# Attention on one core: more buffers behind the reciprocals and the outputs, the next head's loads spread over the groups, another order on TensorE

## What is computed

```python
def fox_attend(q, k, v, cq, ck, pos_q, pos_k):
    scale = HEAD_DIM ** -0.5
    s = jnp.einsum('bqhd,bkhd->bhqk', q, k).astype(jnp.float32) * scale
    decay = jnp.transpose(cq, (0, 2, 1))[:, :, :, None] - jnp.transpose(ck, (0, 2, 1))[:, :, None, :]
    mask = pos_k[None, :] <= pos_q[:, None]
    s = jnp.where(mask[None, None], s + decay, NEG_INF)
    p = jax.nn.softmax(s, axis=-1)
    return jnp.einsum('bhqk,bkhd->bqhd', p.astype(v.dtype), v)
...
    merged = jnp.concatenate([rms_norm(o_attn, g_attn_out), rms_norm(o_conv, g_conv_out)], axis=-1)
    x = x + rms_norm(merged @ w_o, g_post_mix)
```

## Time and profile before

| | us |
|---|---|
| median of 3 runs | 2822.99 |
| lowest, highest | 2822.49, 2825.99 |
| the profiled execution, its own time | 2823.09 |
| its span, first to last instruction | 2821.3 |
| PE busy in the span | 2691.7 (95%) |
| DVE, ACT, POOL busy | 1523.6, 1116.0, 1422.2 |
| granted TensorE clock, mean | 0.981 |

### The profile page before, as it was taken

How to read it: one execution, slowest core, us unless ns; L and a number is a source line. 1 busy time by engine, 2 the same in 40 slices (tenths; PEclk the granted TensorE clock), 3 DMA queues, 4 the chain that set the end, 5 groups by cost and what they waited for, 6 DMA issues and landing times.

```text
span 2821.3 us, 41366 instructions
## 1 busy us (share of the span) xinstructions
PE 2691.7 (95%) x14796; PEld 2403.9 (85%) x14796; DVE 1523.6 (54%) x2594; ACT 1116.0 (40%) x2065; POOL 1422.2 (50%) x912
## 2 busy tenths in 40 slices
PE   9999999998788888999999999999999999999998
PEld 8999999997666667788889898888988898889986
DVE  5333433347666668566533434655655565555554
ACT  3201201117666666544423333443333344333333
POOL 3233334311323322577467777765665577656664
PEclk9999999999899899999999999999999999999999
DMA  6634535664554543467735446621122163221213
GB/s 200 196 108 130 167 96 161 205 174 116 137 149 128 145 134 119 155 208 201 225 116 189 170 147 213 241 90 59 65 68 74 59 261 120 66 68 59 74 59 105
DMA packets 295665, 385.17 MB, mean 137 GB/s; under 512 B 24744, under 2 KB 240752, under 8 KB 291440
## 3 DMA queue, kind: packets, MB, share of 16 engines
q1 hardware_dynamic: 256352, 328.68, 37.8%
q0 software_dynamic: 13920, 35.13, 3.7%
q10 hardware_dynamic: 25264, 19.66, 2.2%
HBM read 276.76 MB, written 106.40 MB: 136 GB/s over the span
## 4 chain that ended last, share of the span: by engine, by line
PE 45%; POOL 2%; DVE 1%; DMA 1%; issue 1%; ACT 0%; SPq 0%; DVEq 0%; POOLq 0%
PE dn_bank L2969 17%; PE up_bank L2945 14%; PE dn_bank L2925 7%; PE up_bank L2900 7%; POOL m_y L2480 1%; POOL m_w_up L2429 1%; DMA m_raw_up<-in_w_up 0%; DMA m_x<-scratch_x 0%; DVE m_raw_up L2721 0%; DVE m_y L2826 0%; DVE m_t L2721 0%; POOL m_u L2472 0%; ACT m_junk L2622 0%; DVE m_y L2780 0%; POOL m_w_dn L2465 0%
## 5 line engine op out<-in xcount | busy, mean ns | idle before, releaser
L2969 PE MATMUL dn_bank<-m_w_dn,m_u 128*128 128x512 f32 x2304 | 542.4, 395 | 1.6 <-POOL m_w_dn L2465 1.6
L2969 PEld LDWEIGHTS dn_bank<-m_w_dn,m_u 128*128 128x128 f32 x2304 | 432.3, 188 | 103.6 <-POOL m_w_dn L2465 1.9
L2945 PE MATMUL up_bank<-m_h,m_w_up 128*128 128x384 f32 x2688 | 472.7, 336 | 7.5 <-DVE m_stage L2735 4.4
L2945 PEld LDWEIGHTS up_bank<-m_h,m_w_up 128*128 128x128 f32 x2688 | 467.1, 188 | 11.7 <-issue 5.0
L2782 DVE TENSOR_TENSOR m_y<-dn_bank,m_y 128x1024 f32<-128x1024 f32 x168 | 205.8, 1225 | 283.1 <-PE dn_bank L2969 283.1
L509 POOL TENSOR_TENSOR w_lo<-w_raw,w_hi 128x1024 fp32r<-128x1024 f32 x72 | 175.8, 2446 | 343.0 <-DVE w_hi L723 343.0
L2472 POOL TENSOR_TENSOR m_u<-m_stage,m_u 128x384 fp32r<-128x384 f32 x128 | 141.5, 1126 | 290.5 <-ACT m_u L2611 290.5
L2429 POOL TENSOR_TENSOR m_w_up<-m_raw_up,m_w_up 128x512 fp32r<-128x512 f32 x128 | 192.3, 1522 | 62.7 <-ACT m_w_up L2579 62.7
L1439 ACT ACTIVATE p_hi<-t_bank 128x512 fp32r<-128x512 f32 (+1 forms) x336 | 167.6, 527 | 137.8 <-PE t_bank L1526 94.2
L939 PE MATMUL proj<-ha_hi,w_hi 128*128 128x384 f32 (+1 forms) x640 | 212.2, 332 | 0.0
L1490 DVE TENSOR_TENSOR p_lo<-t_bank,p_hi 128x512 fp32r<-128x512 f32 (+1 forms) x336 | 189.1, 596 | 39.3 <-ACT p_hi L1439 38.2
(11 more groups left out here) (291 smaller groups left out, 5844.3 us busy)
## 6 DMA issues: line engine op xcount, KB each, us to landing
m_raw_up<-in_w_up SPq DMA_DIRECT2D x48, 1024.0 KB, 5.3
m_raw_dn<-in_w_down SPq DMA_DIRECT2D x47, 1024.0 KB, 4.9
w_raw<-in_w_in SPq DMA_DIRECT2D x72, 512.0 KB, 4.0
scratch_h_pairs<-m_pieces POOLq DMA_DIRECT2D x12, 1792.0 KB, 8.4
m_h<-scratch_h_pairs SPq DMA_DIRECT2D x14, 1536.0 KB, 11.8
nck<-scratch_ncum SPq DMA_DIRECT2D x8, 1312.0 KB, 7.9
scratch_v_hl<-vhl SPq DMA_DIRECT2D x20, 512.0 KB, 2.7
q_hi<-scratch_q_hi SPq DMA_DIRECT2D x16, 528.0 KB, 7.5
```

Of the source, the lines that this page charges most:

```text
L2945: mm = pe.matmul(out, w_up[:, j, wp, k, :], hidden_rows(g, j, hp, k), start=(k == 0 and p == 0), stop=(k == KH - 1 and p == 2))
L2969: mm = pe.matmul(bank[:, cols], part, wd[:, wp, b, cols], start=(b == 0 and p == 0), stop=(b == 1 and p == len(passes) - 1))
```

## The change

`o_t` and the scales get four buffers by using both halves of the 128 partitions, the transposed reciprocals six slots. SP runs `store_scales` and `load_scales` of a group first, then a part of the next head's loads, the store of group k-1, and another part: q_hi and q_lo with g = 0, nothing with the extra group, k_hi and k_lo with g = 1, the decay row and the values with g = 2, nothing with g = 3. The pieces of w_o are loaded and stored from POOL's queue, right after a close. PE ranks scores before turns, ACT an output before an exponential.

```diff
-A_BUFS = 2
+A_BUFS = 4
+R_BUFS = 6
-FIRST_CHOICE = {"pe": "TSV", "dve": "TS", "act": "TMO"}
+FIRST_CHOICE = {"pe": "STV", "dve": "TS", "act": "TOM"}
...
-        o_t = sb("o_t", [P, A_BUFS, 2, 512])
-        scales = sb("att_scales", [P, 2, 512])
+        o_t = sb("o_t", [P, A_BUFS // 2, 2, 512])
+        scales = sb("att_scales", [P, A_BUFS // 2, 512])
...
-        rtotal = sb("rtotal", [P, 2, 32])
-        rtotal_t = sb("rtotal_t", [P, 2, 32])
+        rtotal = sb("rtotal", [P, 32])
+        rtotal_t = sb("rtotal_t", [P, R_BUFS, 32])
...
-        scales_loaded = [sem(f"scales_loaded{i}") for i in range(2)]
+        scales_loaded = [sem(f"scales_loaded{i}") for i in range(A_BUFS)]
...
+        def half_of(q, i):
+
+            a = q.k % A_BUFS
+            return o_t[HD * (a % 2):HD * (a % 2) + HD, a // 2, i, 0:q.wide]
+
+        def scale_of(q):
+
+            a = q.k % A_BUFS
+            return scales[HD * (a % 2):HD * (a % 2) + HD, a // 2, 0:wide(q)]
...
+                    sp.dma_start(pieces[b], rtotal_t[32 * b:32 * b + q.n, q.k % R_BUFS, :]).then_inc(rtotal_stored, 16)
...
-                if q.k >= 2:
-                    sp.wait_ge(att_done, q.k - 1)
+                if q.k >= A_BUFS:
+                    sp.wait_ge(att_done, q.k - A_BUFS + 1)
...
+                sp.dma_start(scale_of(q), line.to_broadcast([HD, wide(q)])).then_inc(scales_loaded[q.k % A_BUFS], 16)
...
+                sp.dma_start(dr["attn_t"][q.head * HD:(q.head + 1) * HD, q.rows], half_of(q, 0)[:, 0:wide(q)]).then_inc(att_stored[q.k % A_BUFS], 16)
...
-            def load_piece(k):
-                sp.wait_ge(w_split, 2 * k)
-                sp.wait_ge(w_stored, 32 * k)
-                sp.dma_start(w_piece[:, :].bitcast(F32), front.piece("w_o", k)).then_inc(w_loaded, 16)
-
-            def store_piece(k):
-                sp.wait_ge(w_split, 2 * k + 2)
-                sp.dma_start(front.piece("w_o_hi", k), w_piece_hi[:, :].bitcast(F32)).then_inc(w_stored, 16)
-                sp.dma_start(front.piece("w_o_lo", k), w_piece[:, :].bitcast(F32)).then_inc(w_stored, 16)
...
             def fetch(head, at):
 
                 par = head % 2
-                if head >= 2 and at == 0:
-                    sp.wait_ge(used, P_BUFS + groups[GROUPS_OF * (head - 1) - 1].products[-1].at + 1)
+                lines = bass.ds(head * HD, HD)
                 if at == 0:
                     sp.wait_ge(blank, 2)
-                    load_queries_keys(sp, dr, head, q_hi[par], q_lo[par], k_hl[par], qk_loaded[par])
-                elif at == 1:
+                    if head >= 2:
+                        sp.wait_ge(used, P_BUFS + groups[GROUPS_OF * (head - 1) - 1].products[-1].at + 1)
+                if at in (0, 1):
+                    tile, name = ((q_hi, "q_hi"), (q_lo, "q_lo"))[at]
+                    for half in range(2):
+                        sp.dma_start(tile[par][HD * half:HD * half + HD, 0:ROWS].bitcast(F32), dr[name][lines, :]).then_inc(qk_loaded[par], 16)
+                elif at in (4, 5):
+                    part, name = at - 4, ("k_hi", "k_lo")[at - 4]
+                    sp.dma_start(k_hl[par][HD * part:HD * part + HD, :].bitcast(F32), dr[name][lines, :]).then_inc(qk_loaded[par], 16)
+                elif at == 6:
                     load_decay(sp, dr, head, nck[par], nck_loaded[par])
-                elif at == 2:
+                elif at == 7:
                     load_values(sp, dr, head, v_hl[par], v_loaded[par])
 
             front.load_gains(sp)
             for q in groups:
-                if q.head < HEADS - 1:
-                    fetch(q.head + 1, q.k % GROUPS_OF)
...
                 store_scales(q)
                 load_scales(q)
-                k, at = divmod(q.k - W_FIRST, W_EVERY)
-                if 0 <= k < KB and at == 0:
-                    load_piece(k)
-                if 0 <= k < KB and at == 2:
-                    store_piece(k)
+                ahead = q.head < HEADS - 1
+                if ahead:
+                    fetch(q.head + 1, 2 * (q.k % GROUPS_OF))
                 if q.k:
                     store(groups[q.k - 1])
+                if ahead:
+                    fetch(q.head + 1, 2 * (q.k % GROUPS_OF) + 1)
...
             def close(q):
-                place, other = (o_t[0:HD, q.k % A_BUFS, i, 0:wide(q)] for i in range(2))
+                place, other = (half_of(q, i)[:, 0:wide(q)] for i in range(2))
                 pool.wait_ge(o_taken, O_BANKS + q.k + 1)
                 pool.tensor_tensor(place, place, other, ALU.add).then_inc(added, 1)
                 pool.wait_ge(added, q.k + 1)
-                pool.wait_ge(scales_loaded[q.k % 2], 16 * (q.k // 2 + 1))
-                pool.tensor_tensor(place, place, scales[0:HD, q.k % 2, 0:wide(q)], ALU.mult).then_inc(att_done, 1)
+                pool.wait_ge(scales_loaded[q.k % A_BUFS], 16 * (q.k // A_BUFS + 1))
+                pool.tensor_tensor(place, place, scale_of(q), ALU.mult).then_inc(att_done, 1)
+
+            def load_piece(k):
+                pool.wait_ge(w_stored, 32 * k)
+                pool.dma_start(w_piece[:, :].bitcast(F32), front.piece("w_o", k)).then_inc(w_loaded, 16)
...
-                pool.wait_ge(w_stored, 32 * k)
...
+                pool.wait_ge(w_split, 2 * k + 2)
+                pool.dma_start(front.piece("w_o_hi", k), w_piece_hi[:, :].bitcast(F32)).then_inc(w_stored, 16)
+                pool.dma_start(front.piece("w_o_lo", k), w_piece[:, :].bitcast(F32)).then_inc(w_stored, 16)
+
+            pool.wait_ge(blank, 2)
...
                     pool.wait_ge(taken, S_BANKS + ALL_TAKEN)
+                    pool.wait_ge(att_done, q.k)
                     front.set_ones(pool)
                     front.sum_blocks(pool, 0, 0)
                     front.rests(pool, 0, 0)
+                    pool.wait_ge(front.S["c_lo_done"], 1)
                 close(q)
                 k, at = divmod(q.k - W_FIRST, W_EVERY)
+                if 0 <= k < KB and at == 0:
+                    load_piece(k)
                 if 0 <= k < KB and at == 1:
+                    pool.wait_ge(att_done, q.k + 1)
...
+                    act.activation(half_of(q, 0), bank[0:HD, 0:q.wide], ACT.Copy)
+                    act.activation(half_of(q, 1), bank[HD:P, 0:q.wide], ACT.Copy).then_inc(o_taken, 1)
...
-                        dve.reciprocal(rtotal[:, q.k % 2, 0:q.n], total[:, sums(q)]).then_inc(recip_made, 1)
-                        if q.k >= 2:
-                            dve.wait_ge(rtotal_stored, 16 * groups[q.k - 2].stores)
+                        if q.k:
+                            dve.wait_ge(recip_done, q.k)
+                        dve.reciprocal(rtotal[:, 0:q.n], total[:, sums(q)]).then_inc(recip_made, 1)
+                        if q.k >= R_BUFS:
+                            dve.wait_ge(rtotal_stored, 16 * groups[q.k - R_BUFS].stores)
                         dve.wait_ge(recip_made, q.k + 1)
-                        dve.transpose(rtotal_t[:, q.k % 2, :], rtotal[:, q.k % 2, :]).then_inc(recip_done, 1)
+                        dve.transpose(rtotal_t[:, q.k % R_BUFS, :], rtotal[:, :]).then_inc(recip_done, 1)
```

More of the change, by code:

```diff
@@ L1314, in store_scales @@
                 for b in range(wide(q) // (32 * q.n)):
-                    sp.dma_start(pieces[b], rtotal_t[32 * b:32 * b + q.n, q.k % 2, :]).then_inc(rtotal_stored, 16)
+                    sp.dma_start(pieces[b], rtotal_t[32 * b:32 * b + q.n, q.k % R_BUFS, :]).then_inc(rtotal_stored, 16)
             def load_scales(q):
                 sp.wait_ge(rtotal_stored, 16 * q.stores)
-                if q.k >= 2:
-                    sp.wait_ge(att_done, q.k - 1)
+                if q.k >= A_BUFS:
+                    sp.wait_ge(att_done, q.k - A_BUFS + 1)
@@ L1321, in load_scales @@
                 line = dr["rtotal"][q.head:q.head + 1, q.rows]
-                sp.dma_start(scales[0:HD, q.k % 2, 0:wide(q)], line.to_broadcast([HD, wide(q)])).then_inc(scales_loaded[q.k % 2], 16)
+                sp.dma_start(scale_of(q), line.to_broadcast([HD, wide(q)])).then_inc(scales_loaded[q.k % A_BUFS], 16)
             def store(q):
                 sp.wait_ge(att_done, q.k + 1)
-                sp.dma_start(dr["attn_t"][q.head * HD:(q.head + 1) * HD, q.rows], o_t[0:HD, q.k % A_BUFS, 0, 0:wide(q)]).then_inc(att_stored[q.k % A_BUFS], 16)
+                sp.dma_start(dr["attn_t"][q.head * HD:(q.head + 1) * HD, q.rows], half_of(q, 0)[:, 0:wide(q)]).then_inc(att_stored[q.k % A_BUFS], 16)
@@ L1421, in _ @@
                     fetch_weights()
+            pool.wait_ge(att_done, len(groups))
         @block.scalar
@@ L1444, in step @@
                     bank = o_bank[q.k % O_BANKS]
-                    act.activation(o_t[0:HD, q.k % A_BUFS, 0, 0:q.wide], bank[0:HD, 0:q.wide], ACT.Copy)
-                    act.activation(o_t[0:HD, q.k % A_BUFS, 1, 0:q.wide], bank[HD:P, 0:q.wide], ACT.Copy).then_inc(o_taken, 1)
+                    act.activation(half_of(q, 0), bank[0:HD, 0:q.wide], ACT.Copy)
```

(3 more changed lines are left out.)

## The result

The changed kernel takes **2761.7 us** (median of 4 runs, 2758.05 to 2766.99) against 2823.55 us for the kernel before in the same comparison (2822.49 to 2825.99): ratio 0.978 [0.976, 0.980]. It is faster, as forecast, but by 62 us and not by 99. 2761.7 lies above the range of 2700 to 2752.

What follows compares the result with a forecast made beforehand. Bound: attention-stage holes, once per head, from small stores queued behind bulk loads. 2823.1 - 99.0 (holes) - 4 (order) + 4 (decay row) = 2724 us; range 2700 to 2752.

Steps and rivals of the forecast that it cites:

- The bound and the holes: Attention stage: VectorE, TensorE and ScalarE stand once per head because small stores queue behind 3.4 MB of bulk loads.
- The clock of 0.98, the stage of 445 us and the 54 to 55 us a head: Signs expected in the attention stage's later profile: clock 0.98 or more, stage about 445 us, heads 54 to 55 us.
- The term of 99.0 us: Attention stage: gain from removing all holes, 496.4 us down to 397.4 us.
- The yardstick of 54.65 us a head: Attention: length of one head without holes, summed from five transpose intervals of heads 6 and 7.
- The split of the term: Attention's 99.0 us: 71.0 VectorE's wait for reciprocal stores, 14.2 TensorE's second kind of hole, 14 slow clock.
- The order, -4 us: TensorE in attention: scores before turns before outputs gains 4 us, bounded by 10 us gain or an equal loss.
- Rival C: Attention: scores first gains more, 3 us a head, by filling TensorE's hidden slack; 2701 us; chance 0.10.
- The decay row, +4 us: SP's queue: next head's decay row, loaded behind g=2's scales, lands 0.6 us late in seven heads, costing 4 us.
- Rival B: Attention: decay row becomes the new wait, 3 to 4 us a head; 2741 to 2748 us; chance 0.22.
- Its second form: DMA: w_o's pieces on POOL's queue take turns with the decay row, 7.3 us in three heads; 2744 us.
- Rival D: Attention: POOL becomes the bound, waiting in order for w_o's pieces and holding outputs back; slower, 2851 us; chance 0.03.
- Rival E: Attention: reciprocal slots run out again, as SP's store wait outlasts six groups; no gain, 2823 us; chance 0.03.

## Why the prediction was off

**The bound and the holes: right.** The marks set for them stand or miss as follows. No wait of the transpose is left and the holes of 10 us are gone. The clock of 0.98, the stage of 445 us and the 54 to 55 us a head were missed (0.95, about 480, and 55.5 to 62.2 from one g = 2 to the next), by the new waits: with keys and decay row early clock and stage are 0.99 and 438.

**The term of 99.0 us: right.** From the due transpose of g = 1 in head 0 to that of g = 2 in head 7 it was 496.4 us, forecast 397.4 without holes. With old ranking and next to no waits it is 394.3 (639.44 to 1033.73, early keys). The yardstick of 54.65 us a head was 0.7 us long (53.9 here), since it was a single head, and not without a wait: ACT stood for an output buffer between the transposes of g = 1 (1120.12) and g = 2 (1134.96), at a clock of 1.00. The row is of the kernel before:

```profile
1129.47 0.59 ACT L1445 ACTIVATE o_t<-o_bank 64x512 f32<-64x512 f32 x1 [1.81 <-DMA scratch_attn_t<-o_t]
```

That interval was 14.84 us there, and 13.90 us in the same head of the kernel before with four output buffers. The changed kernel takes 640.90 to 1070.22, 429.3 us. So the missing 38 us lie in the term for the decay row, 40 us over its forecast, less 5 us that the order brought beyond its own. The split of the term was looser. It had 14 us for the clock, 1.4 a hole, and the stretch of 0.64 begins at 1063.00, 1.8 us before PE resumed at 1064.82. In the two stretches of 3 us from there, in the kernel before:

```profile
1064.82:1067.82 3.00, 3.00 (x12) 2.70 (x13) 2.87 (x7) 0.77 (x2) 0.78 (x1) 0.50 0.70 171
1067.82:1070.82 3.00, 3.00 (x12) 2.43 (x11) 1.75 (x5) 1.34 (x4) 0.80 (x2) 0.61 0.84 322
```

The clock lost 1.5 + 1.2 = 2.7 us behind this hole, an estimate from the two rows. So what a hole costs in clock could be read before any run.

**How it came about: half right.** I gave the gain to six slots and to four output buffers, each for its own wait. The runs show two independent cures for the transposes' wait: the slots (needed with the loads in a lump) or the spread loads (with two slots they do as well). The four outputs are needed with either.

**The order, -4 us: mis-sized.** It is worth 9 us where nothing waits: a clean head takes 52.8 to 53.7 us in place of 53.9. Rival C had that mechanism, with 23 us, two and a half times what it is. No run tried PE's part of the ranking and ACT's apart.

**The decay row, +4 us: the step that failed.** Its place behind the scales of g = 2, with the keys ahead of it, measured 44.3 us. The working can be checked term by term in the seven heads, counted from the transpose of g = 1:

| | forecast | the change | change, old ranking |
|---|---|---|---|
| `nck` issued | +19.5 | +21.2 | +21.8 |
| first score starts | +27.0 | +28.7 | +29.3 |
| DVE ready for it | +26.4 | +23.9 | +25.9 |
| late by | 0.6 | 4.8 | 3.4 |

Two things were wrong in it. The first is the queue: the row came 1.7 us later than forecast, 2.3 us with the old ranking that the working was made for. `k_hi` goes out at +8.9 to +11.7, about as forecast (+9.3 to +10.3), but the keys take longer. I gave both 7.3 us from the first issue; `k_lo` is issued 1.3 us behind `k_hi` and lands 8.0 us after that (625 to 1105 us: size, median us from issue to landing):

```profile
k_hl<-scratch_k_lo SPq DMA_DIRECT2D x7, 656.0 KB, 8.0
```

So the reciprocals of g = 2 are held longer than 1.6 us: with the old ranking `nck` is issued 7.8 us after their transpose, forecast 4.7, and in the change, where they stand behind both key loads for nearly their whole time, 11.6. The second is the need. I took the moment at which DVE needs the row from the kernel before, +26.4, and costed the order apart from it. The new ranking brings the transpose of g = 2 to +9.4 (it was +14.84) and the next head's first score to +23.9. The last column weighs the two: the queue alone makes DVE wait 3.4 us a head (23.9 us of the 33.6), the ranking adds 1.4. Two edits priced one by one met in one margin that was already negative. The order of DVE's instructions could be read before any run.

And the lateness is paid twice. PE stands 31.7 + 1.9 us for `nck` and `k_lo` in the change and 3.7 us for `nck` with both early, which makes 29.9 of the 44.3 us. The other 14.4 are near what the clock rows give. In the first 3 us behind each of five holes it is 0.50, a loss of 1.5 us; in the next 3 us the five lose 1.2, 1.35, 0.54, 1.17 and 1.5 us; the sixth hole costs 3 x 0.29 + 3 x 0.28 = 1.7 us. Together 7.5 + 5.8 + 1.7 = 15.0 us. I had priced 1.4 us of clock for each old hole, and for the new wait nothing. That the clock makes up these 14.4 us is worked out, and no run tried it by itself.

**Rival B** is what happened. Its range of 2741 to 2748 counted 3 to 4 us a head and left out the clock; it took 44.3 / 7 = 6.3 us a head. The sign that it named (3 us and more of idle DVE ahead of the first score of heads 1 to 7) came in six of the seven. **Its second form**, the decay row served in turns with the pieces on POOL's queue, did not decide. In head 2 SP issued `nck` at 778.82 and POOL began to issue its 1 MB of stores at 779.64:

```profile
778.82 0.59 SPq L108 DMA_DIRECT2D nck<-scratch_ncum  x1
...
779.64 0.63 POOL L1419 DMA_DIRECT2D scratch_w_o_hi<-wo_piece_hi  x1 [0.30 <-POOL wo_piece L1417]
...
786.41 0.29 DVE L1490 CUSTOM_DVE_ANT_0 scores_a<-s_bank,nck 128x128 f32<-128x128 f32 x1 [4.80 <-issue]
```

DVE had it 7.6 us after its issue, in head 5 beside stores likewise 7.6, and 7.2 to 7.4 in heads 1, 3, 4 and 6, where POOL issued no transfer while it was under way (in head 4 its stores had gone out 2.8 us ahead). Head 0, with no transfer of POOL's near, took 8.5. By the Trainium skill ("DMA: Bandwidth & Descriptors", "Queues, rings and completion order") each DMA engine takes turns between the queues that have work. These rows show 0.2 to 0.4 us at the most for stores beside `nck`, less than the seven heads differ, and not the 7.3 that I worked out. In head 3, the third of the heads that I named, POOL's load of a piece was issued 3.8 us ahead of `nck` (838.39), which took 7.3. No run took the pieces off POOL's queue with all else as in the change, so their move is priced by these rows alone.

**Rival D** shows in a mild form once. A piece loaded beside the queries came late and POOL stood in order for it:

```profile
812.73 0.60 POOL L1407 DMA_DIRECT2D wo_piece<-in_w_o  x1
...
823.76 2.84 POOL L1413 TENSOR_SCALAR wo_piece<-wo_piece,mix_gains 128x1024 f32<-128x1024 f32 x1 [7.01 <-DMA wo_piece<-in_w_o]
```

The longest transfer of this tile took 10.8 us from issue to landing, against 3.9 for the shortest. The close of the next group, SP's store of it at 832.44 and `k_lo` at 832.97 came late with it, and PE waited 1.92 us for `k_lo`. At 16 us it would have held outputs; it never came to that. **Rival E** had no part.

## What to carry to other kernels

A queue that works in order and waits between small transfers gives every bulk load two prices: how long it holds what follows, and how late it lands itself. Write down for each load when it is needed and when it can be issued in the *changed* order, and leave a margin of more than one bulk load; two edits that take from the same margin have to be priced together. And when two buffers guard the same event, test them together: one alone may show no gain, and still be worth 90 us with the other.

## What was not expected of the hardware

- The price of a hole in the clock. After TensorE had stood for 4.6 to 5.6 us, its granted clock was 0.50, the lower of its two levels, for the next 3 us, and 0.50 to 0.82 for 3 more. A hole of 3.59 us was followed by 0.71 and 0.72 in the same stretches, one of 2.37 us by 1.00. By these rows a hole of 5 us cost 7 to 8, an estimate. In the kernel before, behind a hole of 10.70 us, it was 0.50 and 0.61.
- A clock of 1.00 right at the start isn't the end of it: behind the hole of 3.59 us the first product ran at full speed and the turns 2 us later were slow (eight in 1.97 us; later four took 0.63).

```profile
1030.13 0.50 PE L1531 MATMUL s_bank<-k_hl,q_hi 128*128 128x512 f32 x1 [3.59 <-DVE maxes L1490]
...
1031.96 1.97 PE L1547 MATMUL t_bank<-ident,scores_b 128*128 128x128 f32 x8
...
1036.32 0.63 PE L1547 MATMUL t_bank<-ident,scores_b 128*128 128x128 f32 x4
```

- The releaser "issue" can be a DMA. Six of the seven waits for `nck` carried it; the neighbouring row with its name and SP's queue told what it was.
